# Six runs per phase in the first mixer, fifth turned blocks copied by VectorE, and a fifth pair of gate tiles in the projection stage

## The reference, cut to what matters

```python
proj = rms_norm(x, g_mix) @ w_in
qa, ka, va, qb, kb, vb, gate_logits = jnp.split(proj, cuts, axis=-1)
y_a = chunk_band_relbias_attention(qa, ka, va, rel_table) @ w_branch_a   # mixer A: 64-frame chunks, 576-key band
y_b = sliding_window_sink_gqa(rope(qb), rope(kb), vb, sinks) @ w_branch_b  # mixer B: window 128, rotary, sinks
g_a, g_b = jnp.split(jax.nn.sigmoid(gate_logits + b_gate), 2, axis=-1)
x = x + (g_a * y_a + g_b * y_b) @ w_out
gu = rms_norm(x, g_ffn) @ w_gate_up
x = x + (silu(g_part) * u_part) @ w_down
```

## Time and profile before

| | |
|---|---|
| median of 3 runs | 2589.5 us (2589.29 to 2591.73) |
| the profiled execution's own time | 2588.69 us |
| its span, first to last instruction | 2586.9 us |
| TensorE busy | 2557.4 us, 99% |
| VectorE busy | 1823.0 us, 70% |
| ScalarE busy | 1038.8 us, 40% |
| POOL busy | 286.4 us, 11% |
| mean granted TensorE clock | 0.998 |

### The profile page before, as it was taken

One profiled execution on the slowest core, in us unless ns is written; L12 is line 12 of the kernel. 1 busy time (PEld: TensorE's weight loads), 2 busy tenths in 40 slices (PEclk: granted clock), 3 DMA queues, 4 the chain that ended last, 5 costly groups with the idle time before them and its releaser, 6 DMA issues. The chain is left out here.

```text
span 2586.9 us, 35453 instructions
## 1 busy us (share of the span) xinstructions
PE 2557.4 (99%) x12822; PEld 2095.1 (81%) x12822; DVE 1823.0 (70%) x3321; ACT 1038.8 (40%) x2035; POOL 286.4 (11%) x442
## 2 busy tenths in 40 slices
PE   8999999999999999999999999999999999999998
PEld 6888777888888888888778887778888888888886
DVE  8766555644888777768996665555459777776687
ACT  6222466522533333344542225664235333333444
POOL 0000232344000000000000002224430000000000
PEclk9999999999999999999999999999999999999999
DMA  4323543453133233395423345425422233225843
GB/s 149 130 102 114 176 140 118 135 178 115 60 116 109 90 107 122 99 280 162 151 102 117 111 136 160 145 84 179 151 106 92 88 106 118 91 97 169 260 117 126
DMA packets 200332, 336.92 MB, mean 130 GB/s; under 512 B 18672, under 2 KB 79968, under 8 KB 200160
## 3 DMA queue, kind: packets, MB, share of 16 engines
q1 hardware_dynamic: 191936, 311.47, 36.5%
q10 hardware_dynamic: 8224, 23.20, 2.6%
HBM read 240.76 MB, written 92.92 MB: 129 GB/s over the span
## 5 line engine op out<-in xcount | busy, mean ns | idle before, releaser
L1407 PE MATMUL ps<-op_hi,up_hi 128*128 128x512 f32 x1232 | 479.9, 389 | 2.5 <-DVE third_sum L2996 2.5
L1409 PE MATMUL ps<-op_hi,up_lo 128*128 128x512 f32 x1232 | 479.3, 389 | 0.0
L1408 PE MATMUL ps<-op_lo,up_hi 128*128 128x512 f32 x1232 | 479.3, 389 | 0.0
L1407 PE MATMUL ps<-in_hi,up_hi 128*128 128x512 f32 x728 | 285.0, 392 | 2.6 <-DVE up_lo L2491 2.1
L1408 PE MATMUL ps<-in_lo,up_hi 128*128 128x512 f32 x728 | 283.7, 390 | 0.0
L1409 PE MATMUL ps<-in_hi,up_lo 128*128 128x512 f32 x728 | 283.7, 390 | 0.0
L1407 PEld LDWEIGHTS ps<-op_hi,up_hi 128*128 128x128 f32 x1232 | 231.3, 188 | 51.0 <-issue 3.3
L1409 PEld LDWEIGHTS ps<-op_hi,up_lo 128*128 128x128 f32 x1232 | 231.3, 188 | 48.2
L1408 PEld LDWEIGHTS ps<-op_lo,up_hi 128*128 128x128 f32 x1232 | 231.3, 188 | 47.8
L2091 ACT ACTIVATE up_hi<-up_raw 128x512 fp32r<-128x512 f32 x252 | 158.1, 630 | 278.5 <-PE ps L1409 271.6
L1360 POOL CAST w_hi<-w_raw 128x256 fp32r<-128x256 f32 x184 | 81.5, 485 | 1468.0 <-DMA w_raw<-w_lin 1209.9
(11 more groups left out here) (255 smaller groups left out, 4758.1 us busy)
## 6 DMA issues: line engine op xcount, KB each, us to landing
up_raw<-w_gu SPq DMA_DIRECT2D x42, 1024.0 KB, 5.1
act_raw<-ff_saved SPq DMA_DIRECT2D x154, 256.0 KB, 2.8
w_quarter<-w_lin SPq DMA_DIRECT2D x52, 512.0 KB, 4.5
w_raw<-w_lin SPq DMA_DIRECT2D x48, 512.0 KB, 4.2
ff_saved<-ff_block SPq DMA_DIRECT2D x88, 256.0 KB, 2.0
ff_saved<-ff_mix SPq DMA_DIRECT2D x66, 256.0 KB, 2.0
gated<-gates_saved SPq DMA_DIRECT2D x32, 512.0 KB, 4.2
dn<-w_dn_a SPq DMA_DIRECT2D x48, 256.0 KB, 4.0
```

Source lines behind the costliest of these rows:

```text
L1407: pe.matmul(out, w1, x1, start=first, stop=False, skip_group_check=True)
L1408: pe.matmul(out, w1, x0, start=False, stop=False, skip_group_check=True)
L1409: return pe.matmul(out, w0, x1, start=False, stop=last, skip_group_check=True)
```

## The change

- `IN_GATES = 5`: a fifth pair of gate tiles is done in the projection stage (14 pairs). Six gate tiles are left for the mixer stage; among the runs stand 72 steps: group 0: 8, 4, 4 in its first three A runs; the others 2, 2, 1 and then none; B phases 6 and 5, in the last group 4 and 4.
- Mixer A takes its query blocks in the order 0, 3, 1, 2, 4, 5, 6, 7, so that the first two runs (four units each) have five key blocks per head as the wide ones have: six runs per phase.
- Every A run has a fifth block. VectorE copies it (`take_fifth`), at the last unit of the next run, behind that unit's maximum and head copies; before, ScalarE did it for wide units. Its semaphore is `fifth_ready`.
- `turn_values` and the turning of fifth blocks wait for `fifth_ready` of the earlier A runs.
- Head outputs of all runs but the last two go to bank 6, two places; `weigh` waits until all heads of the run before are taken. The buffers of the probabilities and the score banks are laid out anew, and a buffer is reused two runs later.
- The inverses of A phases are turned at later units (`INVERSE_LATER`).
- The last inverse is applied in two operations of 512 columns instead of four of 256; ScalarE's fifth o_hi waits for the next to last gate half in place of `gates_past`.

```diff
-IN_GATES = 4
+IN_GATES = 5
...
+A_ORDER = (0, 3, 1, 2, 4, 5, 6, 7)
...
 def run_start(u):
-    return u & (~7 if unit(u)[0] == "B" else ~3 if u % PHASE < 4 else ~1)
+    return u & (~7 if unit(u)[0] == "B" else ~3 if u % PHASE < PHASE // 2 else ~1)
...
-FILL_A = ((8, 0, 4, 4, 2, 2, 2, 2),) + ((2, 0, 3, 2, 1, 1, 1, 0),) * (GROUPS - 1)
-FILL_B = ((8, 6),) * (GROUPS - 1) + ((4, 4),)
+FILL_A = ((8, 0, 4, 0, 4, 0, 0, 0),) + ((2, 0, 2, 0, 1, 0, 0, 0),) * (GROUPS - 1)
+FILL_B = ((6, 5),) * (GROUPS - 1) + ((4, 4),)
...
-    return weighed + (4 if weighed % UNITS_PER_GROUP == 2 else 0)
+    return weighed if weighed == HELD else weighed + INVERSE_LATER[eight % len(INVERSE_LATER)]
...
+INVERSE_LATER = (2, 0, 8, 6)
...
             def turn_values(L, s, c):
-                if last_wide(run_start(s) - 1) is not None:
-                    pe.wait_ge(turned_ready, L * TURNS + turned_through(last_wide(run_start(s) - 1)))
+                if last_full(run_start(s) - 1) is not None:
+                    pe.wait_ge(fifth_ready, L * FIFTHS + fifths_through(run_start(s) - 1))
...
+                if fifths > 0:
+                    pe.wait_ge(fifth_ready, fifths)
+                pe.wait_ge(v_ready, L * VALUES + values_before(last + 1))
+                final = key_blocks(mixer, unit(first)[3]) - 1
+                for e in range(2):
+                    mm = pe.transpose(last_ps[:, e * P:(e + 1) * P], soft(first + e)[:, final * P:(final + 1) * P], ident[:, :])
+                mm.then_inc(turned, 1)
...
-                taken = L * HEAD_PAIRS + (u // 2 - (1 if p == 1 else 0) if mixer == "A" else run_start(u) // 2 - (2 if p % 4 < 2 else 0))
+                taken = L * HEAD_PAIRS + run_start(u) // 2
...
-                if wide(last):
-                    act.wait_ge(turned, made + 3)
-                    act.activation(probs_t[:, :, HALF:A_COLS], last_ps.rearrange("p (e n) -> p e n", e=2),
-                                   ACT.Copy).then_inc(turned_ready, 1)
...
+            def take_fifth(L, last):
+                dve.wait_ge(turned, L * TURNS + turned_through(last))
+                taken = L * HEAD_PAIRS + weighed_through(last + 1)
+                if taken > 0:
+                    dve.wait_ge(head_done, taken)
+                dve.tensor_copy(probs_t[:, :, HALF:A_COLS], last_ps.rearrange("p (e n) -> p e n", e=2)).then_inc(fifth_ready, 1)
...
                         for u in weighed_in(s - 1):
                             take_heads(L, u)
+                    if s < UNITS and s == run_end(s) and s > run_end(0) and unit(run_start(s) - 1)[0] == "A":
+                        take_fifth(L, run_start(s) - 1)
```

More of the change, by code:

```diff
@@ L305, in quarters_at @@
 def quarters_at(s, afters):
-    return [2 * eight + j for j, after in enumerate(afters) for eight in inverses_at(s, after)]
+    return sorted(2 * eight + j for j, after in enumerate(afters) for eight in inverses_at(s, after))
 def inverses_before(u):
@@ L327, in turned_through, with copied_through, fifths_through, last_full @@
 def turned_through(u):
-    runs = {run_start(v): 3 if wide(v) else 2 for v in range(u + 1)}
+    runs = {run_start(v): 3 if unit(v)[0] == "A" else 2 for v in range(u + 1)}
     return sum(runs.values())
+def copied_through(u):
+    return 2 * len({run_start(v) for v in range(u + 1)})
+def fifths_through(u):
+    return len({run_start(v) for v in range(u + 1) if unit(v)[0] == "A"})
 def scores_through(u):
     return u + 1 + sum(wide(v) for v in range(0, u + 1, 2))
-def last_wide(u):
-    return max((v for v in range(u + 1) if wide(v)), default=None)
+def last_full(u):
+    return max((v for v in range(u + 1) if unit(v)[0] == "A"), default=None)
+def block_place(p):
+    return A_BLOCKS - 1 - p if p < 2 else 0
 HEAD_PAIRS = UNITS // 2
@@ L637, in o_ps @@
         def o_ps(u):
-            mixer, _, _, p = unit(u)
-            if mixer == "A":
-                return bank(6)[:, P if p == 1 else 0:2 * P if p == 1 else P]
+            if u < LAST_UNIT - EIGHT:
+                place = (u - run_start(u)) // 2
+                return bank(6)[:, place * P:(place + 1) * P]
+            p = unit(u)[3]
             return bank(4 if p % 4 < 2 else 6)[:, p % 2 * P:(p % 2 + 1) * P]
@@ L674, in scale @@
             if mixer == "A":
-                x = x_sb[:, g, p * P:(p + 2) * P]
-                return engine.tensor_tensor(x, x, rows[:, :], ALU.mult)
+                other = unit(QUARTER * quarter + 2)[3]
+                x = x_sb[:, g, :].rearrange("p (b n) -> p b n", n=P)[:, p:other + 1:other - p, :]
+                return engine.tensor_tensor(x, x, rows[:, :].rearrange("p (b n) -> p b n", n=P), ALU.mult)
             tile, chunk = GROUPS + g // 2 * 2, chunk_of(g, p)
@@ L681, in turned_to @@
         def turned_to(u):
-            if unit(u)[0] == "A":
-                return probs_t[:, u % 2, P if u % PHASE in (2, 3) else 0:]
+            mixer, _, e, p = unit(u)
+            if mixer == "A":
+                return probs_t[:, e, block_place(p) * P:]
             return probs_t[:, u % EIGHT // 4, u % 4 * P:(u % 4 + 1) * P]
@@ L692, in soft @@
         def soft(u):
[L694 to L700, removed]
+            mixer, _, e, p = unit(u)
+            if mixer == "B":
+                return probs[2 * (p // 4) + e][:, p % 4 * P:(p % 4 + 1) * P]
+            later = u % PHASE // 4 == 1 if u % PHASE < EIGHT else u % 4 > 1
+            return probs[2 * later + e][:, block_place(p) * P:A_COLS]
         def soft_last(u):
[L704 to L707, removed]
+            return run_start(run_start(u) - 1) - 1 if run_start(u) > 0 else -1
         def gain_at(n, k):
@@ L1527, in scores @@
                         pe.wait_ge(keys_loaded[p // 4], 32 * (L * GROUPS + g + 1))
[L1528 to L1536, removed]
+                    if u % PHASE < EIGHT:
+                        for n, (other, e) in enumerate(((0, 0), (2, 1), (2, 0), (0, 1))):
+                            rows = slice(e * HD, (e + 1) * HD)
+                            pair = unit(u + other)[3]
+                            cols = (pair + 1) * P
+                            if n == 3:
+                                pe.wait_ge(scores_done, L * SCORES + scores_through(u - 1) + 1)
+                            pe.matmul(s_ps(u + other + e, cols), qa[g % 2][rows, pair * P:(pair + 1) * P], ka[g % 2][rows, 0:cols],
+                                      start=True, stop=True).then_inc(scores_done, 1)
                         return
-                    pieces = ((0, 0, cols), (1, 0, cols)) if cols <= HALF else ((0, HALF, cols), (1, P, cols), (0, 0, HALF), (1, 0, P))
+                    k0 = (p + 1 - A_BLOCKS) * P
+                    pieces = ((0, HALF, A_COLS), (1, P, A_COLS), (0, 0, HALF), (1, 0, P))
                     for n, (e, c, d) in enumerate(pieces):
@@ L1578, in turn_run @@
                     for u in range(first + e, last + 1, 2):
[L1579 removed]
+                        pair = unit(u)[3]
                         pe.wait_ge(softened, softened_through(L, u))
[L1581 to L1582 removed]
+                        for j in range(min(key_blocks(mixer, pair), A_BLOCKS - 1 - block_place(pair))):
+                            place = block_place(pair) + j
+                            mm = pe.transpose(t_ps[e][:, place * P:(place + 1) * P], soft(u)[:, j * P:(j + 1) * P], ident[:, :])
                     mm.then_inc(turned, 1)
[L1584 to L1588 removed]
+                if fifths > 0:
[5 more added lines that the diff above has]
+                mm.then_inc(turned, 1)
             def weigh(L, u):
@@ L1966, in take_turned @@
                     return
-                cols = 3 * P if last - first == 3 else min(key_blocks(mixer, p) * P, HALF)
                 for e in range(2):
```

54 lines of the change are left out of this document (29 added, 25 removed).

## The result

The changed kernel takes 2629.6 us (median of 4 runs, 2622.6 to 2631.7) against 2589.4 (4 runs, 2587.4 to 2591.7): ratio 1.015, 95% interval 1.0132 to 1.0169. The forecast was 2609.5, range 2599 to 2620: slower, as forecast, but by 40 us and not by 20. The profiled execution has a span of 2626.3 us, 39.4 more than before.

The account below looks back on a forecast made before the run. TensorE's list of work, busy 99% of the span, was taken as the bound. Work removed and added plus new waits summed to +20.0 us on 2588.7, with 0.8 more for the median: 2609.5 us, range 2599 to 2620.

Parts of the forecast that it names:

- (a): Mixer stages: 32 gate steps per layer leave, 0.680 us each, -43.5 us over both layers.
- (b): Projection stages: one more pair of gate tiles, 84 matmuls per layer, +38.1 us over both layers.
- (c): Mixer stages: six runs for seven, one fixed part of the scores less in each of 8 phases, -2.2 us.
- (d): Second B run of groups 0 to 2: gate half ends mid-run, next step waits 1.55 us for VectorE's logit, +9.3 us.
- (e): Second run of groups 1 to 3: TensorE's next scores wait 1.6 us for VectorE's last maximum, 6 times, +9.6 us.
- (f): Group 0, units 4 and 8: turning values waits for VectorE's fifth-block copies, 3.1 and 0.8 us, +7.8 us.
- (g): Unit 10 of groups 1 to 3: rotation step between two maxima, no gate step, 0.15 us, 6 times, +0.9 us.
- heads before weighing: Mixer stages: VectorE's head copies come before TensorE's weighing, clear by 0.4 us or more, so no wait.
- slow clock in the mixer stages: Rival: clock falls in the long wait of (f), about 2 us lost, twice, 2613.5 us; chance 0.08.
- The later inverses: Mixer stages: inverses turned later, with the POOL scaling behind them, have several runs of slack, so no wait.
- Fifth copies at nothing: Mixer stages: most of VectorE's fifth-block copies, 0.39 us each, stand where it waits for the next scores and cost nothing.
- VectorE keeps up: Rival in the wide runs: nothing waits, the loop runs earlier without ScalarE's fifth copies, -7.6 us, 2582; chance 0.04.

Follow-up runs that it names:

- e5_all: Changed kernel with early inverse save, gate halves ending with a run, earlier fifth-block copy in group 0, later rotations in groups 1 to 3: 2585.0 us.
- e2_halves: Changed kernel with FILL_B 8 and 3 in place of 6 and 5, so gate halves end with a run: 2617.4 us.
- e4_save_rot: Kernel of e1_save with rotations of groups 1 to 3 starting at units 6 and 11 instead of 4 and 9, rotary tables one unit later: 2600.5 us.
- e3_fifth: Changed kernel with VectorE's fifth-block copy in runs of four units behind the second maximum instead of the fourth: 2622.3 us.
- e1_save: Changed kernel with turned inverses saved one unit after turning instead of three (last excepted), ahead of the swapped load in SyncE's queue: 2606.5 us.
- e7_runs_alone: Changed kernel with IN_GATES back at 4 and 104 gate steps among the runs, halves ending with a run: 2615.6 us.
- e10_act_alone: Changed kernel with fifth blocks copied by ScalarE instead of VectorE, all else the same: 2622.8 us.
- e6: Kernel before the change with only the fifth pair of gate tiles in the projection stage, 72 gate steps among the runs: 2588.3 us, ratio 0.9994.

## Why the prediction was half right

The steps of the forecast against the two spans, by its own letters:

| step | forecast | measured | from |
|---|---|---|---|
| (a) 64 gate steps | -43.5 | -43.5 | 0.680 a step, as before |
| (b) 168 matmuls | +38.1 | +37.5 | projection stages, some 1.7 of it slow clock |
| (c) a run fewer | -2.2 | -3.3 | e5_all: busy time of four groups 169.96 for 193.4, less 21.76 for the steps, per layer |
| (d) half crosses a run | +9.3 | +7.7 | wait row; gone in e2_halves |
| (e) second run | +9.6 | +5.5 | wait row, six of 0.92; gone in e4_save_rot |
| (f) value transposes | +7.8 | +7.1 | wait row, 2.87 and 0.69; 2.8 in e3_fifth |
| (g) unit 10 | +0.9 | +0.2 | once |
| heads before weighing | 0 | +16.1 | wait row; gone in e1_save |
| slow clock in the mixer stages | 0 (0.08 for +4) | +10.0 | busy time of the windows |
| sum | +20.0 | +37.3 | of 39.4 in the spans |

The 2.1 us left over are no more than what the table of waits may leave out: by starts a gate step behind the logit is 1.45 us late (348.05, with the one before at 346.37 and 0.23 for it) where the row says 1.29, and 0.16 at each of the 23 waits would be 3.7. I worked out only this one.

The total hides that two errors stood against each other: the forecast waits (d) to (g) came to 20.5 us and not 27.6, while 26.1 us of wait and clock were not in the sum at all.

**The step that failed** is "The later inverses, the POOL scaling behind them and the two fewer tiles to split have several runs of slack", and with it "head copies before weighing ... clear by 0.4 us or more". The slack is there for those who use the inverses. But `take_inverse` itself waits, for the save of the one before, and I laid out VectorE's queue without that wait. Before the change inverses are as close as 4.7 us (one turned at 337.41, one at 342.11) and nothing waits: the first one's save is issued 0.8 us after it was taken, and no load that depends on VectorE's next work stands ahead of it.

```profile
337.72 0.28 DVE L2826 COPY inverse_turned<-ps 8x128 f32<-8x128 f32 x1 [0.95 <-PE ps L1626]
338.53 0.32 SPq L1214 DMA_DIRECT2D inverses_saved<-inverse_turned  x1
342.42 0.28 DVE L2826 COPY inverse_turned<-ps 8x128 f32<-8x128 f32 x1
```

The new order closes a ring: VectorE waits for the save, the save for SyncE's swapped load, that load for VectorE's addition, and the addition stands behind the inverse taken just before. Shown by e1_save, which takes that order alone away, and by e7_runs_alone, where it stays without the gate change.

**The clock** was a rival with 0.08, at +2 us twice, for (f) only. It fell there once in two, at 1.6 us, and four times behind the wait that I had not seen, at 8.4. The mechanism was right, its price per time too; the chance came too low, since the missing row (a mid-kernel wait of 3 us) spoke neither way, and the row against it was one execution: behind that same wait of 2.1 us the clock fell in 8 of the 12 profiles. (The Trainium skill, TensorE: Matmul & The Clock Gate, "HAM oscillation", says that idle gaps between bursts bring the clock down again and again. These traces agree: five times in the mixer stages of the changed kernel.)

**(e) was too large**: the chain from first to last maximum took 4.25 us (357.06 to 361.31) and not 4.86. Half of that is one term: I took 0.90 for the rotation's addition between maxima, from the earlier trace rows; it took 0.61, as the other steps. The rest is mostly the four maxima, 1.64 us and not 1.90. (d) was 0.1 to 0.3 us too large each time.

**Fifth copies at nothing** held at the places where they stand in the change (e10_act_alone: maxima 5.4 for 5.7). e3_fifth shows the bound of that: ahead of a last maximum each costs its 0.34. That *VectorE keeps up* (0.04, 2582) was wrong for this kernel, yet VectorE's amount of work was never the bound: with the same work in another order the time is 2585.0.

By parts: the gate pair alone is worth 0 (-2 at the medians), the new runs alone cost 26 us, the rest of the 40 comes with both together (crossed halves 7.7, scores behind maxima 3.4 more, 4.8 more at the heads, 5 more of slow clock, less e6's own 4.2 of waits: 16.7, for 16.5 by the medians). What stays open: the first values in group 0 still wait 0.7 us twice per layer. Earlier turning of them was not tried.

## What to carry to other kernels

When a step is moved closer to its like, look for what it waits for itself: the place it writes to must be read out first, and if that goes through a DMA, the DMA's place in its queue is part of the path. Lay out the queue that issues transfers beside the compute engines' and look for a ring through it; here a save moved ahead of two loads was worth 23 us. And when TensorE is to wait for two microseconds or more in one piece, count a halved clock behind it as likely, 1.5 to 2.8 us each time.

## What the runs showed of the hardware

The granted clock did not follow the length of a wait alone. In eight profiles I read every wait of TensorE over 1.2 us in the mixer stages. Behind none below 2 us there (longest 1.92) did the clock fall. Of 23 between 2.0 and 3.25 us it fell behind 15: behind one of 2.04, and not behind one of 3.25; behind the same wait of 2.87 or 2.88 us it fell in both layers of e1_save, in neither of e4_save_rot, and in one of the changed kernel. Behind all eight from 3.27 to 4.61 it fell. A fall cost 1.5 to 2.8 us of TensorE's time. That none fell below 2 us there is no safe bound: in the first projection stage all twelve profiles have a wait of 1.88 to 1.92 us near 41 us, and behind it the clock fell in seven (in e5_all the starts are then 0.43 us apart, in the changed kernel 0.23); behind the wait of 2.09 to 2.14 us at the start of layer 2's projection it fell in eight. What decides between two executions of the same wait stays open. Runs of one kernel differ with it: the changed kernel's four span 9 us, and the quickest of them (2622.6) has a mean clock of 0.995 where the first two have 0.993; e5_all's eleven, with no such wait in the mixer stages, span 3.

The time of a small save to DRAM depended on what was in flight. The same save of 4 KB took from 1.2 to 4.0 us from its issue to the last update of its semaphore in the changed kernel (30 saves, median 1.9): 1.2 with little ahead of it (380.16), 3.5 right behind 256 KB of swapped loads and 512 KB of rotary table (376.25). So where a place is reused within one or two runs of 3.8 us, both the save's place in its queue and what is issued just before it count.
